# Mean squares through turned 32 x 32 blocks, and the last keys as one weight tile, in a two-layer hybrid encoder

## The reference, cut to what matters

```python
def rmsnorm(x, g):
    y = x * rsqrt(mean(x * x, axis=-1) + 1e-6)
    return y * g
for i in range(2):
    a = rmsnorm(h, g[0])
    m = retention_mixer(a) if i == 0 else rglru_mixer(a)
    h = h + rmsnorm(m, g[1])
    f = conv_ffn(rmsnorm(h, g[2]))
    h = h + rmsnorm(f, g[3])
```

## Time and profile before

| | |
|---|---|
| median of 3 executions | 701.64 us (701.6 to 701.76) |
| profiled execution | 702.21 us, of which 700.4 us span |
| granted TensorE clock, mean | 0.999 of full speed (2.4 GHz) |
| PE busy | 692.7 us, 99% of the span |
| DVE, ACT, POOL busy | 615.1, 518.3, 22.5 us |
| chain that ended last | PE 94%, DVE 5%, issue 1% |
| DMA, 16 engines | 54.4% busy with the weights' queue |

### The profile page before, as it was taken

The page is one execution under the profiler, slowest core; times in us unless marked ns, Lnnn a source line. Parts: engine busy times, 40 slices in busy tenths (PEclk is TensorE's granted clock), DMA queues, the critical chain, the costliest instruction groups (busy, mean ns, idle before and its releaser), DMA issues.

```text
span 700.4 us, 15910 instructions
## 1 busy us (share of the span) xinstructions
PE 692.7 (99%) x6482; PEld 582.2 (83%) x6482; DVE 615.1 (88%) x836; ACT 518.3 (74%) x836; POOL 22.5 (3%) x25
## 2 busy tenths in 40 slices
PE   9999999999999999999999999999999999999996
PEld 7888888888999888888889998888788888885454
DVE  7979887978889899988998989999999999999543
ACT  7486766766575988877788677999788888887431
POOL 0001010100100000000003000000000000000000
PEclk9999999999999999999999999999999999999999
DMA  9965646453581455555589941110445656666821
GB/s 343 319 254 147 249 143 252 135 187 135 189 335 58 145 189 214 198 183 184 204 331 375 357 170 62 62 61 1 181 169 193 240 198 222 202 218 212 260 40 61
DMA packets 48636, 134.44 MB, mean 192 GB/s; under 512 B 30785, under 2 KB 31297, under 8 KB 33345
## 3 DMA queue, kind: packets, MB, share of 16 engines
q1 hardware_dynamic: 48288, 133.33, 54.4%
q10 hardware_dynamic: 288, 0.31, 0.1%
HBM read 129.17 MB, written 1.05 MB: 186 GB/s over the span
## 4 chain that ended last, share of the span: by engine, by line
PE 94%; DVE 5%; issue 1%; ACT 0%; DVEq 0%
PE ps L1694 24%; PE ps L1696 24%; PE ps L1695 24%; PE ps L2146 3%; PE ps L2145 3%; PE ps L2144 3%; PE ps L1741 1%; PE ps L1737 1%; PE ps L1736 1%; PE ps L1835 1%; PE ps L1828 1%; PE ps L1830 1%; PE ps L2084 1%; PE ps L1762 1%; PE ps L1767 1%; PE ps L1922 1%
## 5 line engine op out<-in xcount | busy, mean ns | idle before, releaser
L1694 PE MATMUL ps<-a_hi,w_hi 128*128 128x272 f16 (+1 forms) x1000 | 276.9, 277 | 0.0
L1696 PE MATMUL ps<-a_hi,w_lo 128*128 128x272 f16 (+1 forms) x1000 | 276.9, 277 | 0.0
L1695 PE MATMUL ps<-a_lo,w_hi 128*128 128x272 f16 (+1 forms) x1000 | 276.9, 277 | 0.0
L1015 DVE SCALAR_TENSOR_TENSOR w_lo<-stage,w_hi 128x1024 f16<-128x1024 f32 x205 | 248.2, 1240 | 23.3 <-ACT w_hi L550 22.7
L550 ACT ACTIVATE w_hi<-stage 128x1024 f16<-128x1024 f32 x205 | 208.0, 1047 | 53.3 <-PE ps L1696 21.5
L1696 PEld LDWEIGHTS ps<-a_hi,w_lo 128*128 128x128 f16 x1000 | 97.8, 98 | 16.0
L1695 PEld LDWEIGHTS ps<-a_lo,w_hi 128*128 128x128 f16 x1000 | 97.8, 98 | 15.9
L1694 PEld LDWEIGHTS ps<-a_hi,w_hi 128*128 128x128 f16 x1000 | 97.8, 98 | 15.9
L1694 PE MATMUL ps<-y_hi,w_hi 128*128 128x272 f16 (+3 forms) x496 | 106.1, 242 | 0.0
L1695 PE MATMUL ps<-y_lo,w_hi 128*128 128x272 f16 (+3 forms) x496 | 106.1, 242 | 0.0
L1696 PE MATMUL ps<-y_hi,w_lo 128*128 128x272 f16 (+3 forms) x496 | 106.0, 242 | 0.0
(11 more groups left out here) (286 smaller groups left out, 1077.0 us busy)
## 6 DMA issues: line engine op xcount, KB each, us to landing
stage<-in_chunks SPq DMA_DIRECT2D x118, 1024.0 KB
work<-work SPq DMA_DIRECT2D x96, 32.0 KB, 2.0
stage<-in_chunks SPq DMA_DIRECT2D x6, 256.0 KB
decay_all<-in_decay SPq DMA_DIRECT2D x1, 1056.0 KB, 11.5
out<-sq SPq DMA_DIRECT2D x4, 256.0 KB, 2.0
hT<-in_tokens SPq DMA_DIRECT2D x3, 272.0 KB, 5.4
stage<-in_chunks SPq DMA_DIRECT2D x1, 512.0 KB
mT<-in_gains SPq DMA_DIRECT2D x1, 512.0 KB, 7.5
```

The source lines that it names most:

```text
L1015: dve.scalar_tensor_tensor(out=part(1, c, q), in0=flat(stage, c, q), scalar=W_SCALE, in1=part(0, c, q), op0=ALU.mult, op1=ALU.subtract).th ...
L1694: pe.matmul(o, w_h, x_h, start=start, stop=False)
L1695: pe.matmul(o, w_h, x_l, start=False, stop=False)
L1696: return pe.matmul(o, w_l, x_h, start=False, stop=stop)
```

## The change

1. **Mean squares in blocks.** For the four norms in front of sub-layers and heads 0 to 2, the summed squares are not multiplied as 272 columns. DVE turns them in nine 32 x 32 blocks and sums each block along its rows (`token_blocks`): partition 32 r + j, column b then holds the part of token 32 b + j from the 32 channels of row group r. PE multiplies these nine columns with a tile that has a one wherever row and column agree modulo 32 (`ident_sb[:, P:2P]`), ACT estimates nine columns, and DVE mends nine columns and turns them back with a broadcast read (`rsqrt_blocks`). The last sum of two tiles gets a wait behind it. `stat_k` moves from 2 to 4 (first norm), 2 to 3 (second and third) and 5 to 6 (fourth).
2. **Waits on the way.** In heads 1 to 3 DVE waits for POOL's sum and then runs `token_blocks`, behind the last weights of chunk c + 3. PE waits for `o_turned` in its place. The norms behind sub-layers and head 3 stay as they are, with 1/D for 1/512 and a factor of 2 in the root.
3. **Last keys.** The weight tile of the last key tile now holds the high parts of the 32 keys, their low parts, and zeros (`last_keys`, [128 x (32, 32, 64)], in an unused part of `v_lo`). It is multiplied with the high and the low queries: 4 matmuls per head for 6. Its rows 32 to 63 are the scores of the low key parts. One more DVE operation puts them, times decay, into rows 96 to 127 of `s_hi[:, 2]`, and one more ACT operation a second copy of the high v into rows 96 to 127 of `v_hi[:, 2]` (`v_copy`, in front of which PE now waits with `v_again` before the product of scores and v). One more ACT and one more DVE operation per head make `last_keys`.
4. **First head.** On ACT, `prep(c + 4, 0)` moves behind the high scores, and quarters 0, 1 and 2 stand with `v_copy` in front of the silu. On DVE `prep(c + 4, 2)` moves in front of `v_evict(1)`.
5. The identity that is loaded has 256 columns for 128.

```diff
+            def estimate_blocks(bank, up, n_up, n, size):
+                ...
+                act.activation(rs0[:, 0:TOK_BLOCKS], ps[:, bank, 0:TOK_BLOCKS], ACTF.Abs_reciprocal_sqrt,
+                               scale=1.0 / size, bias=eps_sb[:, 0:1]).then_inc(rs_est, 1)
@@ ACT, head h
                 qk_high(1)
+                act.activation(last_keys[:, :, 0, :], rotq[:, 2:4, T - EDGE:T], ACTF.Copy).then_inc(last_hi, 1)
...
-                prep(c + 4, 0)
-
                 if h:
-                    estimate(HEAD_BANKS[h][0] + 3, 0, gn_up, h, ESTIMATE[("head", h - 1)])
+                    prep(c + 4, 0)
+                    estimate_blocks(HEAD_BANKS[h][0] + 3, gn_up, h, ESTIMATE[("head", h - 1)], HEAD_V)
...
+                def v_copy():
+                    act.activation(v_hi4[R_KEY:R_KEY + EDGE, 2], vs[2][0:EDGE], ACTF.Identity,
+                                   bias=vsum[0:EDGE, 2, 1:2]).then_inc(v_again, 1)
+
+                if h == 0:
+                    prep(c + 4, 0)
+                    prep(c + 4, 1)
+                    v_copy()
+                    prep(c + 4, 2)
                 act.wait_ge(g_out, h + 1)
                 act.activation(gT, gT, ACTF.Silu, scale=-0.5 * UNSCALE).then_inc(g_silu, 1)
                 if h:
                     head_y(h - 1)
-                prep(c + 4, 1)
+                    v_copy()
+                    prep(c + 4, 1)
                 if h == HEADS - 1:
                     head_squares(h)
-                prep(c + 4, 2)
+                if h:
+                    prep(c + 4, 2)
                 prep(c + 4, 3)
@@ DVE
+            def token_blocks(v):
+                flat = v.rearrange("p a t -> p (a t)")
+                turned = flat[:, 2 * T:2 * T + TOK_BLOCKS * BLOCK]
+                link(dve.transpose(turned, flat[:, 0:TOK_BLOCKS * BLOCK]))
+                return dve.tensor_reduce(out=tok_part, in_=turned.rearrange("p (b j) -> p b j", j=BLOCK),
+                                         op=ALU.add, axis=AX_X)
+
+            def rsqrt_blocks(to, bank, n, size):
+                ...
+                link(dve.scalar_tensor_tensor(out=root, in0=est, scalar=1.0 / size, in1=est, op0=ALU.mult, op1=ALU.mult))
+                link(dve.scalar_tensor_tensor(out=root, in0=ps[:, bank, 0:TOK_BLOCKS], scalar=EPS * size, in1=root,
+                                              op0=ALU.add, op1=ALU.mult))
+                link(dve.scalar_tensor_tensor(out=root, in0=root, scalar=3.0, in1=est, op0=ALU.subtract, op1=ALU.mult))
+                dve.transpose(to.rearrange("p (b j) -> p b j", j=BLOCK),
+                              root.unsqueeze(2).to_broadcast([P, TOK_BLOCKS, BLOCK])).then_inc(rs_made, 1)
+                dve.wait_ge(rs_made, n)
...
-                dve.tensor_tensor(sq_sum[:], sq[:, 0, :], sq[:, 1, :], ALU.add).then_inc(sum_h, 1)
+                link(dve.tensor_tensor(sq[:, 0, :], sq[:, 0, :], sq[:, 1, :], ALU.add))
+                token_blocks(sq).then_inc(sum_h, 1)
@@ DVE, head h
                 qk_low(1)
+                dve.tensor_tensor(last_keys[:, :, 1, :], rotq[:, 2:4, T - EDGE:T], qk_hi[:, 2:4, T - EDGE:T],
+                                  ALU.subtract).then_inc(last_lo, 1)
                 for q in range(3 if h else 1, SUB if h else SUB - 1):
                     prep(c + 3, q)
+                if h:
+                    dve.wait_ge(sum_o, h)
+                    token_blocks(osq).then_inc(o_turned, 1)
...
                 last.then_inc(s_dec, 1)
+                dve.tensor_tensor(s_hi[R_KEY:P, 2, :], ps[EDGE:2 * EDGE, A + 2, 0:T],
+                                  decay_sb[EDGE:2 * EDGE, h, 2 * P - T + 2 * EDGE:2 * P + 2 * EDGE], ALU.mult)
                 if h:
-                    rsqrt(rs, A + 3, 0, ESTIMATE[("head", h - 1)])
+                    rsqrt_blocks(rs, A + 3, ESTIMATE[("head", h - 1)], HEAD_V)
...
                     prep(c + 4, 1)
+                    prep(c + 4, 2)
                     if h == 0:
                         v_evict(h + 1)
-                    prep(c + 4, 2)
@@ PE
-                    pe.matmul(ps[:, STAT_IN[i], t0:T], ones_sb[:, 0, :], sq_sum[:, t0:T], start=True,
+                    pe.matmul(ps[:, STAT_IN[i], 0:TOK_BLOCKS], ident_sb[:, P:2 * P], tok_part, start=True,
                               stop=True).then_inc(ms_up, 1)
...
+                pe.wait_ge(last_set, 1)
+                pe.wait_ge(last_hi, h + 1)
+                pe.wait_ge(last_lo, h + 1)
+                for k in range(2):
+                    both = last_keys[:, k].rearrange("p l a -> p (l a)")
+                    pe.matmul(ps[:, A + 2, 0:T], both, qk_hi[:, k, :], start=k == 0, stop=False)
+                    mm = pe.matmul(ps[:, A + 2, 0:T], both, qk_lo[:, k, :], start=False, stop=k == 1)
                 mm.then_inc(s_up, 1)
...
                 pe.wait_ge(vlo_made, h + 1)
+                pe.wait_ge(v_again, h + 1)
                 pe.wait_ge(slo_made, h + 1)
...
-                    mm = pe.matmul(ps[:, A + e, 0:T], v_hi[0:R_LO + EDGE, 2, col], s_hi[0:R_LO + EDGE, 2, :],
+                    mm = pe.matmul(ps[:, A + e, 0:T], v_hi[:, 2, col], s_hi[:, 2, :],
```

More of the change, by code:

```diff
@@ L378, in build @@
         vlo_made = sem("vlo_made")
+        v_again = sem("v_again")
+        last_hi = sem("last_hi")
+        last_lo = sem("last_lo")
+        last_set = sem("last_set")
         g_out = sem("g_out")
@@ L550, in prep, with estimate @@
                 act.activation(part(0, c, q), flat(stage, c, q), ACTF.Copy, scale=W_SCALE).then_inc(whi_made, 1)
-            def estimate(bank, t0, up, n_up, n):
+            def estimate(bank, t0, up, n_up, n, times=1.0):
                 act.wait_ge(up, n_up)
@@ L1016, in prep, with rsqrt @@
                                          op0=ALU.mult, op1=ALU.subtract).then_inc(wlo_made, 1)
-            def rsqrt(to, bank, t0, n):
+            def rsqrt(to, bank, t0, n, times=1.0):
                 dve.wait_ge(rs_est, n)
-                link(dve.tensor_tensor(rs1[:, t0:T], rs0[:, t0:T], rs0[:, t0:T], ALU.mult))
-                link(dve.scalar_tensor_tensor(out=rs1[:, t0:T], in0=ps[:, bank, t0:T], scalar=EPS,
+                if times == 1.0:
+                    link(dve.tensor_tensor(rs1[:, t0:T], rs0[:, t0:T], rs0[:, t0:T], ALU.mult))
+                else:
+                    link(dve.scalar_tensor_tensor(out=rs1[:, t0:T], in0=rs0[:, t0:T], scalar=times, in1=rs0[:, t0:T],
+                                                  op0=ALU.mult, op1=ALU.mult))
+                link(dve.scalar_tensor_tensor(out=rs1[:, t0:T], in0=ps[:, bank, t0:T], scalar=EPS / times,
                                               in1=rs1[:, t0:T], op0=ALU.add, op1=ALU.mult))
@@ L1320, in _ @@
                     dve.wait_ge(decay_landed, 16)
[L1321 to L1324, removed]
+                for n, m, first_key in ((0, P, 0), (1, P, P), (2, EDGE, T - EDGE)):
+                    last = dve.tensor_tensor(sT[0:m, n, :], ps[0:m, A + n, 0:T],
+                                             decay_sb[0:m, h, 2 * P - first_key:2 * P - first_key + T], ALU.mult)
                 last.then_inc(s_dec, 1)
+                dve.tensor_tensor(s_hi[R_KEY:P, 2, :], ps[EDGE:2 * EDGE, A + 2, 0:T],
+                                  decay_sb[EDGE:2 * EDGE, h, 2 * P - T + 2 * EDGE:2 * P + 2 * EDGE], ALU.mult)
                 if h:
-                    rsqrt(rs, A + 3, 0, ESTIMATE[("head", h - 1)])
+                    rsqrt_blocks(rs, A + 3, ESTIMATE[("head", h - 1)], HEAD_V)
                 else:
@@ L1357, in _ @@
             c = RET_OUT
-            rsqrt(rs, Y, 0, ESTIMATE[("head", HEADS - 1)])
+            rsqrt(rs, Y, 0, ESTIMATE[("head", HEADS - 1)], D / HEAD_V)
             head_y(HEADS - 1)
@@ L1924, in head_norm @@
             def head_norm(h, bank):
-                pe.wait_ge(sum_o, h + 1)
                 if h == HEADS - 1:
+                    pe.wait_ge(sum_o, HEADS)
                     pe.wait_ge(o_gated, HEADS)
-                pe.matmul(ps[:, bank, 0:T], ones_sb[:, 1, :], osq[:, 0, :], start=True,
-                          stop=True).then_inc(gn_up, 1)
+                    o, ones, sums = ps[:, bank, 0:T], ones_sb[:], osq[:, 0, :]
+                else:
+                    pe.wait_ge(o_turned, h + 1)
+                    o, ones, sums = ps[:, bank, 0:TOK_BLOCKS], ident_sb[:, P:2 * P], tok_part
+                pe.matmul(o, ones, sums, start=True, stop=True).then_inc(gn_up, 1)
             def heads(k):
@@ L2233, in constants @@
 def constants():
-    ident = np.eye(P, dtype=np.float32)
+    ident = np.concatenate([np.eye(P), np.tile(np.eye(BLOCK), (P // BLOCK, P // BLOCK))], 1).astype(np.float32)
     d = D // HEADS
```

69 lines of the change are left out of this document (42 added, 27 removed).

## The result

The changed kernel took **702.67 us** in the median (702.41 to 702.96, 20 executions), against 701.64 us (701.31 to 702.12, 20 executions) before: ratio 1.0013, 95% interval 1.0007 to 1.0019. That is 1.0 us more: the interval lies above 1, so the slowdown is real, though smaller than the 1.4 us that the prediction takes as no change. The profiled execution took 702.96 us, with a span of 701.2 us for 700.4.

The account below looks back on a forecast made before the run. PE, busy 99% of the span, was taken as the bound. Taken from PE 2.8 us (6 x 0.23 + 0.93 + 0.5), given back 3.5 (0.9 + 1.8 + 0.8): net +0.7 on 701.64, so 702.3 us; range over the cases 700.4 to 703.5.

Parts of the forecast that it names:

- A nine-column mean: Seven means of squares on PE: 0.23 us each for 0.46, range 0.02 to 0.23, saving 0.23 each.
- Last norm: At 520 us PE's wait of 0.2 us for the sum goes and the mean is 0.24 shorter: gain 0.5 us.
- Rival D: Nine-column means stay at 0.46 us, so blocks save PE nothing: 703.0 us; chance 0.21 together with C.
- DVE's part: Per norm, the sum is ready 0.95 us later and the root takes 0.3 less: DVE 0.65 us later behind it.
- First norm: v out at 25.4 us, PE wanting it at 25.56: gain 0.23 us, margin 0.1, no wait.
- Second head: The copy makes the v turn 0.65 us later, at 95.7, PE wanting it at 94.73: PE waits 0.9 us.
- rival A: Only the fourth head's copy costs; second head's v transfers come earlier, recurrent sub-layer has more slack: 700.6 us; chance 0.22.
- Third head: v turn 0.45 us earlier by scores, 0.65 later by copy, margin 0.6 used up: wait about 0, gain 0.46.
- Fourth head: PE's product with v waits 1.8 us for the copy standing behind `head_y` on ACT; none comes back.
- Rival B: All added work is covered, also the fourth head's copy: 698.8 us, down to 698 with cheaper means; chance 0.08.
- C: Second head's v transfers come late through the first head's ACT order: 703.0 to 703.6 us; chance 0.21 together with D.
- Recurrent sub-layer: Behind the third norm both evictions move 0.65 us later, PE's need 0.23 earlier: PE waits 0.8 us.

Follow-up runs that it names:

- the keys with the copy moved: Kernel before plus only the last keys' full weight tile, with the v rows' copy right behind the split of v: 700.77 us, ratio 0.9987.
- keys alone: Kernel before plus last keys' tile, copy and first head's order as in the change, mean squares as before: 704.4 us, ratio 1.0035; run again 705.64 us.
- copy later: Changed kernel with the fourth head's v rows' copy one weight split later on ACT: 704.61 us.

## Why the prediction was right, and where its terms were not

The forecast was +0.7 us on the median by saving 2.8 and giving back 3.5; measured were +1.0, by about 3.4 and 4.4. Sign, mechanism and the largest term stood. Both sums were too small, by 0.6 and 0.9 us, and that the errors nearly cancel is luck. By its own last line the prediction also missed in one point, as PE waits in a place that it does not name.

- **A nine-column mean, 0.23 taken, 0.14 measured.** The range had it (0.02 to 0.23). I took the 96-column rows as bounded by the weight loads. The records of these loads are indeed long, 190 ns each for the means in the heads against 98 for float16, but two of them are longer than the 0.14 us that the pair of matmuls takes, so they run beside the matmuls ahead. The Trainium skill, "TensorE: Matmul & The Clock Gate", section "Weight-path perf modes", says that FP32 weights don't get the fast load; these two lengths agree, and what I drew from it, that a short mean stays at 0.23, does not hold. Seven times 0.09 makes 0.6 us.
- **Scores, 0.93.** Measured 1.0 by the keys with the copy moved. Right.
- **Last norm, gain 0.5.** PE's lag behind the kernel before falls there from 1.29 to 0.75 us. Right. Rival D, means at the old 0.46, is out by this and by the 0.14.
- **DVE's part, 0.95 and 0.3.** The sum behind its wait, 0.48 from start to start (18.12 to 18.60), turn 0.51 and reduction 0.37 (18.60 to 19.48): 0.88 + 0.11. Root: 3 x 0.20 + 0.5 (22.08 to 23.21). Right. The Trainium skill, "VectorE: DVE Perf Modes", section "Rules for kernel authors", warns of the reduction; 0.455 us for 288 elements agrees with the estimate made from its 1x rate, and here it costs as much as an addition of that size.
- **First norm, no wait forecast; 0.56 and 0.13.** The step that failed. I followed the chain of the norm (sum, mean, root, v turn) with its margin of 0.1 us and did not look at what DVE had queued behind the later sum: `prep(1, 1)`, of which PE wants the low half at 20.2. Moving that split ahead removed the wait. Nor did the margin of 0.1 hold: v was out at 25.79, not 25.4, and PE waited 0.13 for it. With the first wait removed, v is out 4.33 us after the mean starts (20.79 to 25.12), for the 4.2 forecast, and PE, with the shorter mean, would want it after 4.31, for 4.36; PE's start lies another 0.1 behind the turn's end.
- **Second head, 0.9; measured 0.34.** The v turn ended only 0.30 us later, not 0.65, as the 20 transfers were done 1.0 us earlier (ACT's wait at 74.08, for 75.11 before): half of rival A's mechanism. And PE came 0.33 us later than forecast (95.06 for 94.73), the waits of the first norm less the shorter means and the early start.
- **Third head, about 0; measured 0.34.** The copy costs its chain 0.86 us, not 0.65, against the margin of 0.6: the weight split behind it used to overlap the end of `y_hi` by 0.1 us and starts after the copy's end now.
- **Fourth head, 1.8; measured 2.03.** Place, engine and order as forecast (ACT 32 x 512 behind `head_y`), with PE there at 164.16 and not 164.7, and the copy done at 166.1 and not 166.5. Rival B is out, and C too: the transfers were earlier.
- **Recurrent sub-layer, 0.8; measured 0.92**, in two pieces. The size was right and what PE waits for was not: it is the low half of the convolved x rows, one step before the second eviction that I read.

## What to carry to other kernels

In a kernel whose bound engine never rests, a saving counts in full only if every helper operation that it brings is issued ahead of what that engine waits for; one 0.7 us copy in the wrong place of a queue cost 2.0 us, nearly three times its length, and in the right place nothing that shows. When an operation grows, read the queue behind it and not only the chain in front of it: the two large waits of the blocks went, all but 0.14 us, by moving one weight split past its neighbours. And a long wait may cost more than its length (here those of 2.15 and 2.97 us did in some executions, that of 2.03 us in none), so the longest waits are the first to mend.

## What the runs showed of the hardware that was not expected

- After a pause of PE of 2.15 us (keys alone) and of 2.97 us (copy later), with PE busy throughout the microseconds before, the granted clock was 0.5, 1.2 GHz, for some 3 us, in both profiles of the first kernel (falling 0.9 to 1.2 us after PE had begun again) and in that of the second (falling during the pause); after 2.03 us it was 1.00. It added 1 to 2 us, and not in every execution.
- A pair of float32 matmuls of nine columns takes 0.14 us together, from its start to that of the next matmul, at weight load records of 190 ns each.
- A block turn of 288 elements takes 0.48 us, with a plain read (L1066) as with a broadcast one (L1078).
